# Three score products and the recurrence gates on 64 rows of the array instead of 128

## The chip, the cores and the metric

The program runs on one core of a Trainium2 chip. The metric is the device time of one execution in microseconds (us), as the median of three runs. Engines are named as in the profile: PE (TensorE, matmul), PEld (its weight loads), DVE (VectorE), ACT (ScalarE), POOL (GpSimd), SP (SyncE, which issues the weight DMAs).

## What is computed

A block of three layers over x of 256 positions by 1024 features, all in float32: a retention layer, a latent attention layer (16 heads) and a hybrid layer (a gated recurrence beside a sparse attention, then a feed-forward). Four products in it matter here; each sums over 64 features:

```python
# latent attention: 16 heads, 128 features of their own and 64 rotary ones, whose key is shared by all heads
sc = (jnp.einsum('bqhd,bkhd->bhqk', qn_i, k_nope)
      + jnp.einsum('bqhr,bkr->bhqk', qr_i, k_rope)).astype(jnp.float32) * scale
...
# recurrence gates: 16 blocks of 64 features, two matrices a block
xb = x.reshape(x.shape[:-1] + (RNN_BLOCKS, RNN_BLOCK_DIM))
y = jnp.einsum('btnd,nde->btne', xb, w)
...
# indexer: 8 heads of 64, one shared key
rel = jax.nn.relu(jnp.einsum('bqhd,bsd->bqhs', iqc, ik).astype(jnp.float32))
...
# sparse attention: 16 heads of 64, 4 key heads
s = jnp.einsum('bqgrd,bqkgd->bqgrk', qg, k_sel).astype(jnp.float32) * scale
```

## The kernel before

Each engine's program is written out by hand in its final order; engines meet through semaphores (`wait_ge`, `then_inc`). The large weights come as 148 units. For each unit SP loads `w_raw`, ACT copies it to `w_hi_ring` (`act_hi`, L932), DVE subtracts to get `w_lo_ring` (`dve_lo`, L1373), three units ahead of PE, and PE multiplies in three passes a tile (`mm3`, L337 to L339). Between the units PE does the small float32 products; PSUM has 8 banks of 512 columns.

Latent attention: 8 pairs of heads (`pe_pair`). While pair p is projected, pair p-1 is attended: the scores of head 0 into bank 5 after the gate unit, its transposes (`pe_turn_p`) into bank 6 two units later, then the scores of head 1 into bank 5. A head has four score matmuls (`pe_scores`, L612 and L613): 128 and 256 keys, each over the 128 own features and then over 128 rows of which 64 belong to the other head; `b_kr` holds the rotary key twice, with zeros in the other head's rows.

Hybrid layer, `pe_hybrid`: a loop of 16 units n=0 to 15, each 48 matmuls. Before units 0 and 1 stand four indexer heads each (L739, key padded with zeros in `c_ikz`), before units 2 and 3 four tiles of recurrence gates each (L746 and L747: one matmul per matrix, two 64-feature blocks on the diagonal of a 128x128 weight padded with zeros). After units 6, 8, 10 and 12 come the attention scores of key head g=0 to 3 (L759 and L761, keys padded in `c_kz`), after units 8, 10, 12, 14 the transposes of the exponentials of g=0 to 3 (L776), after the odd units 9 to 15 the values (L787). These transposes wait for `sc_exp`, the end of the exponentials on ACT (`act_attention_exps`, L1332), which wait for the maxima on DVE (`dve_attention_scores`, L1935 to L1944).

ACT's program in the same loop, for each n: the copy of unit n+3, then the indexer's relu (n<2), or the sigmoids of the gates (n=2, 3, L1315 and L1316, one activation of 128x256 each), or the recurrence's exp and tanh (n=4, L1246 and L1250) and sqrt (n=5), then what unit n itself left in its bank (gelu, L1263, for n<4; tanh, L1269, for n=4 to 11), then for n=6, 8, 10, 12 the exponentials. PE waits before unit n=2 to 5 for the gelu of unit n-2, before n=6 to 13 for the tanh of unit n-2. A change of function costs a table load.

Of the kernel before, what the change touches and what calls it, by code (L numbers as in the profile page):

```python
# [6 lines left out]
ACT = mybir.ActivationFunctionType  # L7
# [68 lines left out]
    "c_sq", "c_total", "c_h0", "c_h1", "c_drain_a", "c_drain_v", "c_kw_hi", "c_kw_lo", "c_sp_in", "c_sp_exp", "c_zeros",  # L76
# [110 lines left out]
def place_latent(k):  # L187
# [12 lines left out]
    k.b_kr = k.place("b_kr", [P, 2, S])  # L200
# [8 lines left out]
def place_hybrid(k):  # L209
# [6 lines left out]
    k.c_kz = k.place("c_kz", [P, HKV, S])  # L216
    k.c_iqT = k.place("c_iqT", [P, IH // 2, S])
    k.c_ikz = k.place("c_ikz", [P, 2, S])
# [6 lines left out]
    k.c_rgw = k.place("c_rgw", [P, 2, KD, P])  # L225
# [372 lines left out]
def pe_scores(k, pair, h):  # L598

    T, s, ps, par = k.T, k.s, k.ps, pair % 2  # L600
    i = 2 * pair + h
    if h == 0:
        T.wait_ge(s["b_qn"], pair + 1)
        T.wait_ge(s["b_kn"], pair + 1)
        T.wait_ge(s["b_qr"], pair + 1)
        T.wait_ge(s["b_v"], pair + 1)
        T.wait_ge(s["b_kr"], 1)
    if i:
        T.wait_ge(s["b_masked"], i)
# [28 lines left out]
def pe_pair(k, pair):  # L638
# [13 lines left out]
    else:  # L652
        pe_scores(k, pair - 1, 0)
# [36 lines left out]
def pe_attention_hooks(k):  # L690
# [13 lines left out]
    def last_split():  # L704
# [3 lines left out]
            1: [lambda: pe_scores(k, last, 0)],  # L708
            2: [lambda: pe_turn_p(k, last, 0), lambda: pe_scores(k, last, 1), outputs_split],
# [97 lines left out]
def pe_hybrid(k):  # L807
# [41 lines left out]
    for n in range(16):  # L849
# [7 lines left out]
        elif n in (2, 3):  # L857
# [3 lines left out]
            for c in range(4 * (n - 2), 4 * (n - 2) + 4):  # L861
                pe_recurrence_gates(k, 16 + c, c)
# [221 lines left out]
def act_pT(k, pair, h):  # L1084
# [4 lines left out]
    A.activation(k.b_pT[:, h, :], k.ps[:, 6, 0:3 * P], ACT.Copy).then_inc(s["b_pT"], 1)  # L1089
# [35 lines left out]
def act_attention_output(k):  # L1125
# [19 lines left out]
    act_dma(k, "rgw_in", k.c_rgw[:, :, :, :].rearrange("p a k n -> p (a k n)"), d["rg_w"])  # L1145
# [15 lines left out]
def act_hybrid(k):  # L1161
# [72 lines left out]
    for n in range(16):  # L1234
# [50 lines left out]
def act_to_features(k, i, name, t0):  # L1285
# [320 lines left out]
def dve_key_rotary(k):  # L1606
# [7 lines left out]
    for n in range(2):  # L1614
# [552 lines left out]
```

## Time and profile before

| | us |
|---|---|
| median of 3 runs | 912.55 (912.54 to 913.08) |
| profiled execution, device time | 912.84 |
| its span on the core | 911.5 |
| PE busy in the span | 903.1 (99%) |
| PEld, DVE, ACT, POOL busy | 812.8, 594.4, 494.7, 79.6 |
| granted TensorE clock, mean | 0.999 |

Outside the span lie 1.3 us (912.84 less 911.5). A row of the timeline gives the start of a group, its length, its engine, the line, the operation, output and inputs (moving operand first, then the weights), the array size, the moving shape, and in brackets the idle time before it. A float32 matmul stands as two records (x2), each with a weight load of its own. PE's records overlap: what counts is the distance from one start to the next.

### The profile page before, as it was taken

The page shows a single profiled execution, that of the slowest core. Times are in us where ns is not written, and L with a number is a line of the kernel's source. Part 1 is how long each engine was busy: PE and PEld are TensorE (multiplying, and loading weights), DVE is VectorE, ACT ScalarE, POOL GpSimd, SP SyncE. Part 2 cuts the span into 40 slices and gives each one's busy share as a digit, 9 for nine tenths or more (in the row PEclk, how much of TensorE's full clock was granted, in tenths as well). Part 3 has the DMA queues.
Part 4 walks back from the last instruction along what each step waited for, and adds up shares of the span by engine and source line. Part 5 has one row for each costly group of instructions (what it writes and reads, how often), then busy time and mean ns, then how long its engine had stood idle before and what let it go on. Part 6 is the DMA issues. An engine that isn't in the chain of part 4 may idle for free.

```text
span 911.5 us, 13482 instructions
## 1 busy us (share of the span) xinstructions
PE 903.1 (99%) x5671; PEld 812.8 (89%) x5671; DVE 594.4 (65%) x795; ACT 494.7 (54%) x624; POOL 79.6 (9%) x60
## 2 busy tenths in 40 slices
PE   9999999999999999999999999999999999999998
PEld 8798887888899999999877899999999888888887
DVE  5876656569866666666477788766657665566441
ACT  6444454436766666664437576877754355446330
POOL 0010110000001111111000000222200012211000
PEclk9999999999999999999999999999999999999999
DMA  9835464543544443354465444242244535445720
GB/s 351 324 124 177 182 228 155 194 150 122 185 185 145 145 145 145 145 186 185 160 236 198 171 146 178 93 140 93 97 181 164 206 139 185 164 161 212 253 110 24
DMA packets 24829, 154.65 MB, mean 170 GB/s; under 512 B 3136, under 2 KB 3520, under 8 KB 9024
## 3 DMA queue, kind: packets, MB, share of 16 engines
q1 hardware_dynamic: 22880, 148.97, 45.4%
q10 hardware_dynamic: 1728, 4.28, 1.5%
q8 instruction: 45, 0.74, 0.3%
q0 software_dynamic: 160, 0.52, 0.1%
q14 instruction: 16, 0.13, 0.0%
HBM read 152.72 MB, written 1.05 MB: 169 GB/s over the span
## 4 chain that ended last, share of the span: by engine, by line
PE 88%; ACT 5%; DVE 4%; issue 2%; DMA 1%; SPq 0%; ACTq 0%
PE ps L337 23%; PE ps L339 23%; PE ps L338 22%; PE ps L388 7%; PE ps L391 3%; ACT w_hi_ring L932 1%; ACT c_p L1332 1%; PE ps L612 1%; PE ps L613 1%; PE ps L633 1%; DMA w_raw<-in_a_w_in 1%; PE ps L410 1%; PE ps L517 1%; PE ps L623 1%; PE ps L787 1%
## 5 line engine op out<-in xcount | busy, mean ns | idle before, releaser
L1373 DVE TENSOR_TENSOR w_lo_ring<-w_raw,w_hi_ring 128x2048 fp32r<-128x2048 f32 x146 | 341.8, 2353 | 201.3 <-ACT w_hi_ring L932 201.1
L932 ACT ACTIVATE w_hi_ring<-w_raw 128x2048 fp32r<-128x2048 f32 x146 | 277.4, 1909 | 109.8 <-PE ps L339 104.3
L337 PE MATMUL ps<-xT_hi,w_hi_ring 128*128 128x256 f32 x520 | 149.8, 288 | 0.6 <-DVE w_lo_ring L1379 0.5
L339 PE MATMUL ps<-xT_hi,w_lo_ring 128*128 128x256 f32 x520 | 147.0, 283 | 0.0
L338 PE MATMUL ps<-xT_lo,w_hi_ring 128*128 128x256 f32 x520 | 147.0, 283 | 0.0
L337 PE MATMUL ps<-w_hi_ring,xT_hi 128*128 128x512 f32 (+1 forms) x272 | 107.5, 395 | 1.4 <-DVE xT_lo L1550 0.6
L339 PE MATMUL ps<-w_hi_ring,xT_lo 128*128 128x512 f32 (+1 forms) x272 | 104.5, 384 | 0.0
L338 PE MATMUL ps<-w_lo_ring,xT_hi 128*128 128x512 f32 (+1 forms) x272 | 104.2, 383 | 0.0
L337 PEld LDWEIGHTS ps<-xT_hi,w_hi_ring 128*128 128x128 f32 x520 | 99.6, 192 | 2.2 <-issue 1.5
L338 PEld LDWEIGHTS ps<-xT_lo,w_hi_ring 128*128 128x128 f32 x520 | 99.6, 192 | 0.7
L339 PEld LDWEIGHTS ps<-xT_hi,w_lo_ring 128*128 128x128 f32 x520 | 99.6, 192 | 0.0
L388 PE MATMUL ps<-xw,w_hi_ring 128*128 128x512 f32 x256 | 80.5, 396 | 0.0
L337 PEld LDWEIGHTS ps<-w_hi_ring,xT_hi 128*128 128x128 f32 x272 | 51.1, 188 | 12.6 <-issue 2.3
L339 PEld LDWEIGHTS ps<-w_hi_ring,xT_lo 128*128 128x128 f32 x272 | 51.0, 188 | 9.8
L338 PEld LDWEIGHTS ps<-w_lo_ring,xT_hi 128*128 128x128 f32 x272 | 51.1, 188 | 9.5 <-issue 1.0
L391 PEld LDWEIGHTS ps<-xw,w_lo_ring 128*128 128x128 f32 x256 | 48.1, 188 | 11.4
L391 PE MATMUL ps<-xw,w_lo_ring 128*128 128x256 f32 x256 | 50.3, 278 | 0.0
L337 PE MATMUL ps<-w_hi_ring,c_fT_hi 128*128 128x512 f32 x128 | 49.9, 390 | 0.0
L339 PE MATMUL ps<-w_hi_ring,c_fT_lo 128*128 128x512 f32 x128 | 49.8, 389 | 0.0
L338 PE MATMUL ps<-w_lo_ring,c_fT_hi 128*128 128x512 f32 x128 | 49.8, 389 | 0.0
L337 PE MATMUL ps<-b_qlatT_hi,w_hi_ring 128*128 128x256 f32 x144 | 41.9, 291 | 0.0
L339 PE MATMUL ps<-b_qlatT_hi,w_lo_ring 128*128 128x256 f32 x144 | 40.4, 281 | 0.0
(327 smaller groups left out, 1704.9 us busy)
## 6 DMA issues: line engine op xcount, KB each, us to landing
w_raw<-in_a_w_in SPq DMA_DIRECT2D x22, 1024.0 KB, 5.0
w_raw<-in_w_ff_in SPq DMA_DIRECT2D x16, 1024.0 KB, 4.8
w_raw<-in_w_ff_out SPq DMA_DIRECT2D x16, 1024.0 KB, 4.8
w_raw<-in_b_w_uq SPq DMA_DIRECT2D x16, 576.0 KB, 4.5
w_raw<-in_a_w_out SPq DMA_DIRECT2D x8, 1024.0 KB, 4.9
w_raw<-in_b_w_gate SPq DMA_DIRECT2D x8, 1024.0 KB, 4.8
w_raw<-in_kv_w_up SPq DMA_DIRECT2D x8, 1024.0 KB, 4.8
w_raw<-in_b_w_out SPq DMA_DIRECT2D x8, 1024.0 KB, 4.8
```

The lines of the kernel that those rows point to most:

```text
L337: k.T.matmul(out, lh, rh, start=start, stop=False, skip_group_check=True)
L338: k.T.matmul(out, lh, rl, start=False, stop=False, skip_group_check=True)
L339: return k.T.matmul(out, ll, rh, start=False, stop=stop, skip_group_check=True)
L388: k.T.matmul(out, wh[:, n, c * P:(c + 1) * P], xw[:, n, :, :].rearrange("p a s -> p (a s)"), start=n == 0, stop=False, skip_group_check=True)
L391: m = k.T.matmul(out[:, 0:S], wl[:, n, c * P:(c + 1) * P], xw[:, n, 0, :], start=False, stop=n == KD - 1, skip_group_check=True)
L410: m = k.T.transpose(bank[:, (2 * n + t) * P:(2 * n + t + 1) * P], src(t, 2 * pair + n), k.ident[:, :])
L517: m = T.matmul(k.ps[:, 0, cols], k.a_qk[:, 2 + n, e * P:(e + 1) * P], k.a_qk[:, n, e * P:2 * P], start=e == 0 and n == 0, stop=n == 1, ski ...
L612: T.matmul(out, k.b_qn[:, par, h, qs], k.b_kn[:, par, h, keys], start=q == 0, stop=False, skip_group_check=True)
L613: m = T.matmul(out, k.b_qr[:, par, qs], k.b_kr[:, h, keys], start=False, stop=True, skip_group_check=True)
L623: m = T.transpose(k.ps[:, 6, n * P:(n + 1) * P], k.b_p[:, h, n * P:(n + 1) * P], k.ident[:, :])
L932: k.A.activation(k.hi[:, u % RING, :], k.raw[u % RING][:, :], ACT.Copy).then_inc(k.s["w_hi"], 1)
L1373: k.V.tensor_tensor(k.lo[:, u % RING, :], k.raw[u % RING][:, :], k.hi[:, u % RING, :].bitcast(F32), ALU.subtract).then_inc(k.s["w_lo"], 1)
```

## The change

The products over 64 features address only 64 of the 128 rows: rows 0 to 63 or 64 to 127, where the operands lie. No zeros are stored, and the memsets of `b_kr`, `c_kz` and `c_ikz` go. Matmuls on opposite halves are issued in turn, with outputs in different banks.

- Latent attention: the scores of both heads are issued together, before the first q unit, into banks 5 and 6; first the four matmuls over 128 rows, then four over 64. The transposes go back into the same head's bank.
- Indexer: a head uses the half its features lie in.
- Gates: a 64-feature block has both matrices side by side, 64 columns each, as one 64-row by 128-column weight. Two banks serve two tiles (`pair`); the two halves of a tile come out in different banks, so the sigmoids work on 64 partitions each, twice as many of them.
- Sparse attention: heads keep their order; `c_kT` holds each key head in both halves, eight copies of 64x256 instead of four. Eight matmuls alternate between the halves, and before (r, q) = (1, 0) PE waits for its own (2, 0) (`sc_even`), since both write bank 4.

```diff
-    k.b_kr = k.place("b_kr", [P, 2, S])
+    k.b_kr = k.place("b_kr", [P, 2, S])[:, 0, :]
...
-    k.c_kz = k.place("c_kz", [P, HKV, S])
+    k.c_kT = k.place("c_kT", [P, HKV, S])
     k.c_iqT = k.place("c_iqT", [P, IH // 2, S])
-    k.c_ikz = k.place("c_ikz", [P, 2, S])
+    k.c_ikT = k.place("c_ikT", [P, 2, S])[:, 0, :]
...
-    k.c_rgw = k.place("c_rgw", [P, 2, KD, P])
+    k.c_rgw = k.place("c_rgw", [P, 2, KD, P])[:, 0, :, :]
...
-def pe_scores(k, pair, h):
+def pe_scores(k, pair):
 
     T, s, ps, par = k.T, k.s, k.ps, pair % 2
-    i = 2 * pair + h
-    if h == 0:
-        T.wait_ge(s["b_qn"], pair + 1)
-        T.wait_ge(s["b_kn"], pair + 1)
-        T.wait_ge(s["b_qr"], pair + 1)
-        T.wait_ge(s["b_v"], pair + 1)
-        T.wait_ge(s["b_kr"], 1)
-    if i:
-        T.wait_ge(s["b_masked"], i)
-    for q, cols in enumerate((slice(0, P), slice(P, 3 * P))):
-        out, qs, keys = ps[:, 5, cols], slice(q * P, (q + 1) * P), slice(0, (q + 1) * P)
-        T.matmul(out, k.b_qn[:, par, h, qs], k.b_kn[:, par, h, keys], start=q == 0, stop=False, skip_group_check=True)
-        m = T.matmul(out, k.b_qr[:, par, qs], k.b_kr[:, h, keys], start=False, stop=True, skip_group_check=True)
-    m.then_inc(s["b_scored"], 1)
+    T.wait_ge(s["b_qn"], pair + 1)
+    T.wait_ge(s["b_kn"], pair + 1)
+    T.wait_ge(s["b_qr"], pair + 1)
+    T.wait_ge(s["b_v"], pair + 1)
+    T.wait_ge(s["b_kr"], 1)
+    if pair:
+        T.wait_ge(s["b_pT"], 2 * pair)
+    spans = [(slice(q * P, (q + 1) * P), slice(0, (q + 1) * P), cols) for q, cols in enumerate((slice(0, P), slice(P, 3 * P)))]
+    for h in range(2):
+        for qs, keys, cols in spans:
+            T.matmul(ps[:, 5 + h, cols], k.b_qn[:, par, h, qs], k.b_kn[:, par, h, keys], start=qs.start == 0, stop=False,
+                     skip_group_check=True)
+    for qs, keys, cols in spans:
+        for h in range(2):
+            rows = slice(h * ROPE, (h + 1) * ROPE)
+            m = T.matmul(ps[:, 5 + h, cols], k.b_qr[rows, par, qs], k.b_kr[rows, keys], start=False, stop=True,
+                         skip_group_check=True)
+            if qs.start:
+                m.then_inc(s["b_scored"], 1)
 
 
 def pe_turn_p(k, pair, h):
     T, s, i = k.T, k.s, 2 * pair + h
     T.wait_ge(s["b_p"], i + 1)
-    if i:
-        T.wait_ge(s["b_pT"], i)
     for n in range(3):
-        m = T.transpose(k.ps[:, 6, n * P:(n + 1) * P], k.b_p[:, h, n * P:(n + 1) * P], k.ident[:, :])
+        m = T.transpose(k.ps[:, 5 + h, n * P:(n + 1) * P], k.b_p[:, h, n * P:(n + 1) * P], k.ident[:, :])
     m.then_inc(s["b_pturned"], 1)
...
     else:
-        pe_scores(k, pair - 1, 0)
+        pe_scores(k, pair - 1)
...
         pe_turn_p(k, pair - 1, 0)
-        pe_scores(k, pair - 1, 1)
...
-            1: [lambda: pe_scores(k, last, 0)],
-            2: [lambda: pe_turn_p(k, last, 0), lambda: pe_scores(k, last, 1), outputs_split],
+            1: [lambda: pe_scores(k, last)],
+            2: [lambda: pe_turn_p(k, last, 0), outputs_split],
...
+def half_rows(n):
+    return slice(64 * (n % 2), 64 * (n % 2) + 64)
 def pe_index_scores(k, i, hd):
-    bank = pe_small_bank(k, i)
+    bank, rows = pe_small_bank(k, i), half_rows(hd)
     for q, cols in enumerate(QCOLS):
-        m = k.T.matmul(bank[:, cols], k.c_iqT[:, hd // 2, q * P:(q + 1) * P], k.c_ikz[:, hd % 2, 0:(q + 1) * P],
+        m = k.T.matmul(bank[:, cols], k.c_iqT[rows, hd // 2, q * P:(q + 1) * P], k.c_ikT[rows, 0:(q + 1) * P],
                        start=q == 0, stop=True, skip_group_check=True)
     m.then_inc(k.s["small_mm"], 1)
 
 
-def pe_recurrence_gates(k, i, n):
-    bank = pe_small_bank(k, i)
-    k.T.matmul(bank[:, 0:S], k.c_rgw[:, 0, n, :], k.c_xc[:, n, :], start=True, stop=True, skip_group_check=True)
-    k.T.matmul(bank[:, S:2 * S], k.c_rgw[:, 1, n, :], k.c_xc[:, n, :], start=False, stop=True,
-               skip_group_check=True).then_inc(k.s["small_mm"], 1)
+def pe_recurrence_gates(k, i, pair):
+    banks = [pe_small_bank(k, i + n) for n in range(2)]
+    for c in range(2):
+        for n in range(2):
+            rows, tile = half_rows(n), 2 * pair + c
+            m = k.T.matmul(banks[n][:, c * S:(c + 1) * S], k.c_rgw[rows, tile, :], k.c_xc[rows, tile, :], start=c == 0, stop=True,
+                           skip_group_check=True)
+            if c == 1:
+                m.then_inc(k.s["small_mm"], 1)
 
 
 def pe_attention_scores(k, g):
...
         T.wait_ge(s["sc_in"], g)
     else:
         T.wait_ge(s["small_read"], 24)
-    for r in range(4):
-        tile = 4 * (g // 2) + r
-        T.matmul(ps[:, 4, r * P:(r + 1) * P], k.c_qT[:, tile, 0:P], k.c_kz[:, g, 0:P], start=r == 0, stop=True,
-                 skip_group_check=True)
-        m = T.matmul(ps[:, 5 + r // 2, (r % 2) * S:(r % 2 + 1) * S], k.c_qT[:, tile, P:2 * P], k.c_kz[:, g, :],
-                     start=r % 2 == 0, stop=True, skip_group_check=True)
+    for r, q in ((0, 0), (1, 1), (2, 0), (3, 1), (0, 1), (1, 0), (2, 1), (3, 0)):
+        if (r, q) == (1, 0):
+            T.wait_ge(s["sc_even"], g + 1)
+        rows, tile = half_rows(r), 2 * g + r // 2
+        out = ps[:, 5 + r % 2, (r // 2) * S:(r // 2 + 1) * S] if q else ps[:, 4, r * P:(r + 1) * P]
+        m = T.matmul(out, k.c_qT[rows, tile, q * P:(q + 1) * P], k.c_kT[rows, g, 0:(q + 1) * P],
+                     start=r < 2 if q else r == 0, stop=True, skip_group_check=True)
+        if (r, q) == (2, 0):
+            m.then_inc(s["sc_even"], 1)
     m.then_inc(s["sc_mm"], 1)
...
-            for c in range(4 * (n - 2), 4 * (n - 2) + 4):
-                pe_recurrence_gates(k, 16 + c, c)
+            for pair in range(2 * (n - 2), 2 * (n - 2) + 2):
+                pe_recurrence_gates(k, 16 + 2 * pair, pair)
...
-    A.activation(k.b_pT[:, h, :], k.ps[:, 6, 0:3 * P], ACT.Copy).then_inc(s["b_pT"], 1)
+    A.activation(k.b_pT[:, h, :], k.ps[:, 5 + h, 0:3 * P], ACT.Copy).then_inc(s["b_pT"], 1)
...
         for g in range(HKV):
-            rows = slice(64 * (g % 2), 64 * (g % 2) + 64)
-            m = A.activation(k.c_kz[rows, g, :], bank[rows, (g // 2) * S:(g // 2 + 1) * S], ACT.Copy, scale=hn[rows, 1:2])
+            src = half_rows(g)
+            for n in range(2):
+                m = A.activation(k.c_kT[half_rows(n), g, :], bank[src, (g // 2) * S:(g // 2 + 1) * S], ACT.Copy, scale=hn[src, 1:2])
     else:
-        A.wait_ge(s["c_zeros"], 1)
-        for g in range(2):
-            rows = slice(64 * g, 64 * g + 64)
-            m = A.activation(k.c_ikz[rows, g, :], bank[rows, 0:S], ACT.Copy, scale=hn[rows, 2:3])
+        m = A.activation(k.c_ikT, bank[:, 0:S], ACT.Copy, scale=hn[:, 2:3])
     m.then_inc(s["small_read"], 1)
...
-def act_recurrence_gates(k, i, n):
-    A, s, bank = k.A, k.s, k.ps[:, 4 + i % 4, :]
-    A.wait_ge(s["small_mm"], i + 1)
-    A.activation(k.c_rr[:, n, :], bank[:, 0:S], ACT.Sigmoid, bias=k.vec["rg_ba_2"][:, n:n + 1])
-    A.activation(k.c_ig[:, n, :], bank[:, S:2 * S], ACT.Sigmoid, bias=k.vec["rg_bx_2"][:, n:n + 1]).then_inc(s["small_read"], 1)
+def act_recurrence_gates(k, i, pair):
+    A, s, vec = k.A, k.s, k.vec
+    for n in range(2):
+        A.wait_ge(s["small_mm"], i + n + 1)
+        bank, own, other = k.ps[:, 4 + (i + n) % 4, :], half_rows(n), half_rows(n + 1)
+        for c in range(2):
+            tile, cols = 2 * pair + c, slice(c * S, (c + 1) * S)
+            A.activation(k.c_rr[own, tile, :], bank[own, cols], ACT.Sigmoid, bias=vec["rg_ba_2"][own, tile:tile + 1])
+            m = A.activation(k.c_ig[own, tile, :], bank[other, cols], ACT.Sigmoid, bias=vec["rg_bx_2"][other, tile:tile + 1])
+        m.then_inc(s["small_read"], 1)
 
 
 def head_scale(k, g):
 
-    first = 8 * (g // 2) + g % 2
-    return k.c_qs[:, :, first:first + 7:2]
+    return k.c_qs[:, :, 4 * g:4 * g + 4]
...
-    own.mark(V.memset(k.b_kr[:, :, :], 0.0))
...
-    for n in range(2):
-        rows = slice(n * ROPE, (n + 1) * ROPE)
-        m = V.tensor_tensor(k.b_kr[rows, n, :], k.b_xc[rows, :], k.b_xs[rows, :], ALU.add)
-    m.then_inc(s["b_kr"], 1)
+    V.tensor_tensor(k.b_kr, k.b_xc[:, :], k.b_xs[:, :], ALU.add).then_inc(s["b_kr"], 1)
...
-        m = V.tensor_tensor(q1[:, 2 * half:2 * half + 2, :], ps[:, 5 + half, :].rearrange("p (k s) -> p k s", k=2),
+        m = V.tensor_tensor(q1[:, half:half + 3:2, :], ps[:, 5 + half, :].rearrange("p (k s) -> p k s", k=2),
...
-    G.wait_ge(s["c_kw_lo"], 1)
-    G.memset(k.c_kz[:, :, :], 0.0)
-    G.memset(k.c_ikz[:, :, :], 0.0).then_inc(s["c_zeros"], 1)
...
-    rg = np.zeros((P, 2, KD, P), wa.dtype)
-    for n, w in enumerate((wa, wx)):
-        for half in range(2):
-            rows = slice(64 * half, 64 * half + 64)
-            rg[rows, n, :, rows] = w[half::2].transpose(1, 0, 2)
+    rg = np.empty((P, KD, P), wa.dtype)
+    for half in range(2):
+        rows, other = slice(64 * half, 64 * half + 64), slice(64 * (1 - half), 64 * (1 - half) + 64)
+        rg[rows, :, rows] = wa[half::2].transpose(1, 0, 2)
+        rg[rows, :, other] = wx[half::2].transpose(1, 0, 2)
     out["rg_w"] = rg.reshape(P, -1)
```

PE in the latent attention, pair p-1's scores between the gate unit and the end of the two q units of pair p. `b_kn`, `b_qn` are the own features, `b_kr`, `b_qr` the rotary ones, `b_p` the softmax of a head. Before, with the 54 matmuls of the q units left out:

```order
L612 MATMUL ps<-b_kn,b_qn 128x128 [waits b_v,b_qr,b_kr,b_kn,b_qn]
L613 MATMUL ps<-b_kr,b_qr 128x128
L612 MATMUL ps<-b_kn,b_qn 128x256
L613 MATMUL ps<-b_kr,b_qr 128x256
...
L623 MATMUL ps<-ident,b_p 128x128 [waits b_p]
L623 MATMUL ps<-ident,b_p 128x128 x2
L612 MATMUL ps<-b_kn,b_qn 128x128 [waits b_masked]
L613 MATMUL ps<-b_kr,b_qr 128x128
L612 MATMUL ps<-b_kn,b_qn 128x256
L613 MATMUL ps<-b_kr,b_qr 128x256
```

After, the same stretch:

```order
L611 MATMUL ps<-b_kn,b_qn 128x128 [waits b_v,b_qr,b_kr,b_kn,b_qn]
L611 MATMUL ps<-b_kn,b_qn 128x256
L611 MATMUL ps<-b_kn,b_qn 128x128
L611 MATMUL ps<-b_kn,b_qn 128x256
L616 MATMUL ps<-b_kr,b_qr 128x128 x2
L616 MATMUL ps<-b_kr,b_qr 128x256 x2
...
L626 MATMUL ps<-ident,b_p 128x128 [waits b_p]
L626 MATMUL ps<-ident,b_p 128x128 x2
```

Head 1's scores moved ahead of the q units, and the rotary matmuls of both heads stand in a row of four; the number of matmuls is the same.

ACT in the hybrid loop, n=2: the sigmoids before the gelu of unit 2. `c_rr` and `c_ig` are the two gates. Before:

```order
L1315 ACTIVATE c_rr<-ps,c_columns 128x256 [waits small_mm]
L1316 ACTIVATE c_ig<-ps,c_columns 128x256
L1315 ACTIVATE c_rr<-ps,c_columns 128x256 [waits small_mm]
L1316 ACTIVATE c_ig<-ps,c_columns 128x256
...
L1263 ACTIVATE c_gel<-ps 128x512 [waits w_used]
```

After:

```order
L1337 ACTIVATE c_rr<-ps,c_columns 64x256 [waits small_mm]
L1339 ACTIVATE c_ig<-ps,c_columns 64x256
L1337 ACTIVATE c_rr<-ps,c_columns 64x256
L1339 ACTIVATE c_ig<-ps,c_columns 64x256
L1337 ACTIVATE c_rr<-ps,c_columns 64x256 [waits small_mm]
L1339 ACTIVATE c_ig<-ps,c_columns 64x256
L1337 ACTIVATE c_rr<-ps,c_columns 64x256
L1339 ACTIVATE c_ig<-ps,c_columns 64x256
...
L1282 ACTIVATE c_gel<-ps 128x512 [waits w_used]
```

Eight activations of 128 partitions ahead of the gelu became sixteen of 64, in units 2 and 3 alike.

## Rows read from the trace of the kernel before

**Rows 1.** The page, busy time of each engine.

```profile
PE 903.1 (99%) x5671; PEld 812.8 (89%) x5671; DVE 594.4 (65%) x795; ACT 494.7 (54%) x624; POOL 79.6 (9%) x60
```

**Rows 2.** The page, chain that ended last, by engine.

```profile
PE 88%; ACT 5%; DVE 4%; issue 2%; DMA 1%; SPq 0%; ACTq 0%
```

**Rows 3.** The same chain in order of time, 560 to 690 us: start, length, what.

```profile
560.71 2.62 PE ps L739 x16
...
569.08 0.43 PE ps L746 x2
...
588.01 1.91 ACT w_hi_ring L932
...
591.23 3.32 ACT c_aa L1246 x8
...
605.79 1.81 ACT w_hi_ring L932
...
665.21 2.62 PE ps L787 x24
```

**Rows 4.** Timeline of PE, 286 to 300 us: latent attention, one head's scores.

```profile
289.53 0.38 PE L612 MATMUL ps<-b_kn,b_qn 128*128 128x128 f32 x2
289.75 0.39 PE L613 MATMUL ps<-b_kr,b_qr 128*128 128x128 f32 x2
289.98 0.60 PE L612 MATMUL ps<-b_kn,b_qn 128*128 128x256 f32 x2
290.41 0.59 PE L613 MATMUL ps<-b_kr,b_qr 128*128 128x256 f32 x2
...
290.96 0.28 PE L338 MATMUL ps<-b_qlatT_lo,w_hi_ring 128*128 128x256 f32 x1
```

**Rows 5.** Timeline of PE, 598 to 690 us: the four transposes of exponentials.

```profile
618.74 1.53 PE L776 MATMUL ps<-ident,c_p 128*128 128x128 f32 x12
...
636.90 1.47 PE L776 MATMUL ps<-ident,c_p 128*128 128x128 f32 x12
...
655.39 1.53 PE L776 MATMUL ps<-ident,c_p 128*128 128x128 f32 x12 [0.37 <-ACT c_p L1332]
...
673.33 1.47 PE L776 MATMUL ps<-ident,c_p 128*128 128x128 f32 x12
```

**Rows 6.** Timeline of ACT, 530 to 690 us: last record of each key head's exponentials.

```profile
618.50 0.19 ACT L1332 ACTIVATION_READ_ACCUMULATOR c_p<-c_p,c_few,c_qs 128x1 f32 x1
...
636.08 0.19 ACT L1332 ACTIVATION_READ_ACCUMULATOR c_p<-c_p,c_few,c_qs 128x1 f32 x1
...
655.15 0.19 ACT L1332 ACTIVATION_READ_ACCUMULATOR c_p<-c_p,c_few,c_qs 128x1 f32 x1
...
670.39 0.19 ACT L1332 ACTIVATION_READ_ACCUMULATOR c_p<-c_p,c_few,c_qs 128x1 f32 x1
```

**Rows 7.** The same timeline of ACT: units 1 to 3 of the hybrid loop.

```profile
569.11 0.60 ACT L1263 ACTIVATE c_gel<-ps 128x512 f32<-128x512 f32 x1 [4.45 <-PE ps L339]
...
572.82 0.48 ACT L1315 ACTIVATE c_rr<-ps,c_columns 128x256 f32<-128x256 f32 x1
...
575.87 1.28 ACT L1263 ACT_TABLE_LOAD   x1
578.31 0.60 ACT L1263 ACTIVATE c_gel<-ps 128x512 f32<-128x512 f32 x1 [1.16 <-PE ps L339]
...
587.51 0.60 ACT L1263 ACTIVATE c_gel<-ps 128x512 f32<-128x512 f32 x1 [1.16 <-PE ps L339]
```

**Rows 8.** ACT's half-row activations, instructions of line 1295, then the timeline.

```profile
L1295 ACT ACTIVATE c_kz<-ps,c_columns x4: 470/470/472, 549.7 to 551.1; 64x256 f32<-64x256 f32 x4
...
549.66 1.92 ACT L1295 ACTIVATE c_kz<-ps,c_columns 64x256 f32<-64x256 f32 x4
552.38 1.02 ACT L1231 ACTIVATE c_xc<-ps,c_columns 128x256 f32<-128x256 f32 x2 [0.80 <-PE ps L339]
```

More of the change, by code:

```diff
@@ L74 @@
     "b_pturned", "b_pT", "b_valued", "b_og", "b_oT_hi", "b_oT_lo", "b_qn", "b_cos", "b_sin", "b_qr", "b_kn", "b_v",
-    "c_sq", "c_total", "c_h0", "c_h1", "c_drain_a", "c_drain_v", "c_kw_hi", "c_kw_lo", "c_sp_in", "c_sp_exp", "c_zeros",
+    "c_sq", "c_total", "c_h0", "c_h1", "c_drain_a", "c_drain_v", "c_kw_hi", "c_kw_lo", "c_sp_in", "c_sp_exp", "sc_even",
     "c_ikw_mm", "c_ikw", "c_heads", "c_conv0", "c_conv", "small_mm", "small_read", "ix_acc", "selected",
@@ L1144, in act_attention_output @@
     act_dma(k, "kw_in", k.c_kw_raw[:, :, :].rearrange("p k n -> p (k n)"), d["w_ikw"])
-    act_dma(k, "rgw_in", k.c_rgw[:, :, :, :].rearrange("p a k n -> p (a k n)"), d["rg_w"])
+    act_dma(k, "rgw_in", k.c_rgw.rearrange("p k n -> p (k n)"), d["rg_w"])
     act_hi(k, U_BOUT + 6 + AHEAD)
@@ L1239, in act_hybrid @@
         elif n < 4:
-            for c in range(4 * (n - 2), 4 * (n - 2) + 4):
-                act_recurrence_gates(k, 16 + c, c)
+            for pair in range(2 * (n - 2), 2 * (n - 2) + 2):
+                act_recurrence_gates(k, 16 + 2 * pair, pair)
         elif n == 4:
@@ L1627, in dve_softmax @@
     for q, cols in enumerate(qcols):
-        m = V.tensor_tensor_reduce(out=k.b_p[:, h, cols], in0=ps[:, 5, cols], in1=k.b_mask[:, cols], scale=SCALE_B, scalar=-3.0e38,
+        m = V.tensor_tensor_reduce(out=k.b_p[:, h, cols], in0=ps[:, 5 + h, cols], in1=k.b_mask[:, cols], scale=SCALE_B, scalar=-3.0e38,
                                    op0=ALU.add, op1=ALU.max, accum_out=k.b_sums[:, h, q:q + 1])
@@ L2095, in layout @@
     rnn_x, rnn_g, q, k, v, iq, ik, iw, gates = np.split(w, np.cumsum([DR, DR, D, 256, 256, IH * ID, ID, IH]), 1)
-    group = HC // HKV
-    order = [(t // group * 2 + half) * group + t % group for t in range(HC // 2) for half in range(2)]
-    q = q.reshape(D, HC, DC)[:, order].reshape(D, D)
     out["w_qkvi"] = units(np.concatenate([q, k, v, iq], 1), 4, 512)
@@ L2111, in layout @@
     out["head_norms"] = np.ascontiguousarray(np.stack(norms, 1))
+    out["rg_bx_2"] = np.roll(out["rg_bx_2"], 64, 0)
     out["columns"] = np.ascontiguousarray(np.concatenate([out.pop(name) for name, _ in COLUMNS_C], 1))
     wa, wx = out.pop("rg_wa_2")[0], out.pop("rg_wx_2")[0]
-    rg = np.zeros((P, 2, KD, P), wa.dtype)
-    for n, w in enumerate((wa, wx)):
-        for half in range(2):
-            rows = slice(64 * half, 64 * half + 64)
-            rg[rows, n, :, rows] = w[half::2].transpose(1, 0, 2)
+    rg = np.empty((P, KD, P), wa.dtype)
[3 more added lines that the diff above has]
+        rg[rows, :, other] = wx[half::2].transpose(1, 0, 2)
     out["rg_w"] = rg.reshape(P, -1)
```

## The prediction

> **What bounds the kernel now.** I read the page first: PE is busy 903.1 of 911.5 us, no other engine over 65% [rows 1], and the chain that ended last is 88% PE [rows 2]. So a microsecond taken from PE is worth one, unless another engine stands right behind it. The chain in order of time says where one does: from 588.01 us it leaves PE for ACT and DVE (first the copy of a weight unit, then the recurrence's exp, a later copy) and comes back to PE only at the transposes at 655.39 [rows 3, 5]. PE itself shows 0.37 us of idle time there [rows 5], which hides how close the race is. To measure it I set the end of each key head's exponentials beside the start of PE's transposes of them [rows 5, 6]: for g=0 the last record ends at 618.50 + 0.19 = 618.69 and PE starts at 618.74, slack none; for g=1 636.27 against 636.90, slack 0.6; for g=2 655.34 against 655.39, and PE had waited; for g=3 670.58 against 673.33, slack 2.7. So between unit 3 of the hybrid loop and the third transposes, ACT and DVE set the pace as much as PE does. Before that PE leads: ACT's gelus wait for PE 4.45 us in unit 1 and 1.16 us each in units 2 and 3 [rows 7].
>
> **What 64 rows can save on PE.** A float32 matmul is two records. From start to start a matmul of 128 moving columns takes 0.22 us and one of 256 takes 0.43 [rows 4], so 0.11 and 0.215 a record. The trace of before has no matmul on part of the rows, so what two halves do together has to be bounded. No overlap: nothing is saved. Full overlap of opposite halves: half. I take the middle: records start in order, and the second record of one matmul runs beside the first of the next one on the other half, while the two records of one matmul, on one half, follow each other. I also let no two records start closer than 0.11 us, since the 24 records of values, with only 64 moving columns each, still take 2.62 us, 0.109 each [rows 3], which I read as the time of a weight load.
> - Rotary scores of a pair: before 2 x (0.22 + 0.43) = 1.30 us. After, eight records: 8 x 0.11 = 0.88. Saved 0.42.
> - Indexer, four heads: before 2.62 [rows 3]. Each head ends in a record of 0.215 that the next head's two short ones run beside: 2.62 - 3 x 0.215 = 1.98. Saved 0.64, twice.
> - Gates of a unit: before 8 x 0.43 = 3.44 [rows 3]; after 9 x 0.215 = 1.94. Saved 1.5, twice.
> - Attention scores of a key head: before 4 x (0.22 + 0.43) = 2.6; after, by the weight loads, 16 x 0.11 = 1.76. Saved 0.86, four times.
>
> **Switches.** Going from 128 to 64 rows and back may cost something each time; no row shows it. Below: nothing. Above: what a matmul still takes after the next could start, 0.28 - 0.12 or 0.38 - 0.22 = 0.16 us [rows 4] (the 0.12 is three passes of a unit in 0.36, a 48-matmul unit thus 5.75), plus one uncovered weight load of 0.11, so 0.27. I take 0.11, the load alone, the nearest thing with a row. Two switches go with each group. The Trainium skill ("TensorEngine Tiling (Array Packing)", Key Properties) says that changing the tiling mode drains the engine; no run here shows it. By it alone the switch would be 0.16 and my sum 1.2 us higher.
>
> **Latent attention.** Eight pairs, (0.42 - 0.22) each: -1.6 us. It lies on PE's path: the scores' inputs come from the pair before, through engines that start from PE's own end of the values, so nothing new is waited for. The wait for `b_masked` goes, the new one for `b_pT` is for a copy that PE's values of the pair before already waited for. The softmax of head 0 still has the two q units (54 x 0.12 = 6.5 us) before its transposes; head 1's is early. The DVE memset and the split add are off the path: nothing.
>
> **Hybrid, up to unit 1.** Indexer: 2 x (0.64 - 0.22) = -0.84 us. ACT has eight key copies in place of four and one indexer copy in place of two: five times 0.48 less two, +1.4 us, in front of a convolution drain that ACT was 0.8 us early for [rows 8]; the next gelu had still more room. Nothing on the path. The POOL memsets were long done.
>
> **Hybrid, units 2 and 3: the gates move the bound to ACT.** Before, eight sigmoids lie between 572.82 and the table load at 575.87, 3.05 us [rows 7], some 0.36 apart. After there are sixteen, on 64 partitions. The nearest rows are the four copies of 64x256: 470 ns each, the four in 1.92, so 0.48 apart, with no overlap between them [rows 8]. Sixteen at 0.48 are 7.7 us, 4.65 more in each of the two units. ACT's idle time in them, 1.16 each [rows 7], is used up first: 2 x 4.65 - 2.3 = +7.0 us at the gelu of unit 3. PE arrives 3 us early there and gets nothing for it. From that gelu ACT runs without a gap through the copy at 588.01, the exp at 591.23, tanh, sqrt and their table loads to the copy at 605.79 [rows 3], DVE takes over, and the exponentials of g=0 end at 618.69. All of it starts from the gelu and moves by 7.0. PE waits before units 5 and 6 (gelu of unit 3, tanh of unit 4) and again at the transposes. Lower bound for an activation: 0.36 as for the full-row sigmoids, 16 x 0.36 = 5.8, and ACT is +3.4 late instead of +7.0.
> The Trainium skill ("ScalarE: Activation LUTs", What ACT_TABLE_LOAD costs) has back-to-back activations overlap by about 93 ns; the full-row sigmoids do so, the half-row copies of rows 8 don't. With it the late start would be the smaller one, rival 1 below.
>
> **Hybrid, from there.** The exponentials of g=1 and g=2 follow those of g=0 by 17.6 and 19.1 us [rows 6] on ACT and DVE alone. The scores' saving, 0.86 - 0.22 = 0.64 each, is lost where PE waits: after g=2 PE still stands at +7.0. Between the third and the fourth transposes PE leads again (slack 2.7), and one saving counts: +7.0 - 0.64 = +6.4. The rest of the kernel moves as a whole.
>
> **Sum.** -1.6 - 0.84 + 6.4 = +3.9 us (rounded). The profiled execution took 912.84 and the median is 912.55, 0.3 lower; with the change 912.84 + 3.9 = 916.7, on the median's scale **916.5 us**. With free switches: +7.0 - 0.86 - 1.28 - 3.36 = +1.5, 914.0. With 0.27 a switch: 7.0 - 0.3 - 0.2 + 1.0 = +7.5, 920.1.
>
> **The rivals.**
> 1. *Half-row sigmoids overlap as full-row ones do* (0.36 us). ACT is +3.4 late. With my switch: 3.4 - 0.64 - 0.84 - 1.6 = +0.3, 912.9. With free switches: 3.4 - 5.5 = -2.1, **910.4, faster**. This is the case on the other side: it needs both, sigmoids under about 0.37 us apart and switches near zero. For it: the sigmoids of before. Against: the only half-row rows there are.
> 2. *No overlap of the halves in float32.* PE saves nothing and pays the switches: 7.0 + 0.2 + 0.4 + 1.8 = +9.4, 922.0; with free switches 919.5. For it: two records and two weight loads a matmul, each load 0.11. Against: records and loads already overlap on the full array.
> 3. *Full overlap.* A group takes half: 1.3, 2.6 and 5.2 us (one score group, both indexer groups, eight pairs). With my switch 7.0 - 1.1 - 2.2 - 3.4 = +0.3, 912.8; free, 7.0 - 9.2 = -2.2, 910.4; with sigmoids at 0.36 as well 906.8 to 909.3. It needs a matmul to start beside the whole of the one before; the order of two records each speaks against that. The Trainium skill ("TensorE: Matmul & The Clock Gate", Part 3) gives such starts some 4 ns apart on separate row groups; no run here shows that.
>
> **How the numbers follow.** My forecast, with any switch cost, 0.47; rival 1 0.22; rival 2 0.13; rival 3 0.18. A measurement of this kernel can tell about 0.2%, 1.8 us, from no change. Faster: rival 1 with free switches 0.07, rival 3 in part 0.10, together 0.17. Within 0.2% (910.7 to 914.4): my case with free switches 0.12, rival 1 0.12, rival 3 0.08, together 0.32. Slower: 0.51. The range from 910.5 to 920.6 leaves out most of rival 2 and the best of rival 3, 0.2 in all.
>
> **What would show it.** Half-row sigmoids 0.48 or 0.36 apart in the timeline of ACT; no idle time on ACT ahead of the gelus of units 2 and 3; the gelu of unit 3 later behind that of unit 1 than 18.4 us before, by 7.0. PE idle ahead of units 5 and 6, several us in all, released by ACT. Eight rotary records in 0.9 us and the gap behind them; 1.8 us from the first to the last attention score. Slack between exponentials and transposes near zero for g=0 and g=2. The forecast is wrong if PE shows no idle time ahead of unit 6, or if records on opposite halves don't start beside each other.

## The result and the profile after

The change makes the kernel slower: 915.24 us (median of nine runs, 914.75 to 915.59) against 912.54 (nine runs, 912.24 to 913.30). The ratio is 1.0028, 95% interval 1.0019 to 1.0037. The profiled execution took 915.06 us with a span of 913.7.

The page of the changed kernel, busy times and chain, against [rows 1, 2]:

```profile
PE 897.3 (98%) x5671; PEld 800.8 (88%) x5671; DVE 593.3 (65%) x793; ACT 504.8 (55%) x643; POOL 78.1 (9%) x58
...
PE 85%; ACT 7%; DVE 4%; issue 2%; DMA 1%; SPq 0%; ACTq 0%
```

PE has 5.8 us less to do in a span 2.2 us longer; ACT has 10.1 us more, and its share of the chain went from 5 to 7%. Who waited for whom, PE's waits (total, times, longest), shows two that were not there before:

```profile
PE ps L337 <- ACT c_g L1288: 4.8, 2, 4.5
PE ps L759 <- ACT c_ig L1339: 2.7, 1, 2.7
```

Of the first, 4.5 us stand ahead of unit 6 of the hybrid loop, for the tanh of unit 4. The second is inside the gates of unit 3, whose last tiles need banks that the sigmoids haven't read yet.

**Where ACT's time goes.** The timeline of ACT, units 1 to 3, against [rows 7]:

```profile
565.12 0.60 ACT L1282 ACTIVATE c_gel<-ps 128x512 f32<-128x512 f32 x1 [3.63 <-PE ps L339]
...
568.83 0.47 ACT L1337 ACTIVATE c_rr<-ps,c_columns 64x256 f32<-64x256 f32 x1
569.31 0.47 ACT L1339 ACTIVATE c_ig<-ps,c_columns 64x256 f32<-64x256 f32 x1
569.79 0.47 ACT L1337 ACTIVATE c_rr<-ps,c_columns 64x256 f32<-64x256 f32 x1
...
576.58 1.28 ACT L1282 ACT_TABLE_LOAD   x1
577.87 0.60 ACT L1282 ACTIVATE c_gel<-ps 128x512 f32<-128x512 f32 x1
...
590.62 0.60 ACT L1282 ACTIVATE c_gel<-ps 128x512 f32<-128x512 f32 x1
```

The sixteen sigmoids stand 0.48 us apart and take 7.75 us to the table load (568.83 to 576.58), where eight took 3.05. The gelus of units 2 and 3 no longer wait for PE. The gelu of unit 3 follows that of unit 1 by 25.50 us; before, by 18.40. That is +7.1.

**What the halves do on PE.** Timeline of PE, latent attention. The first two rows show the whole groups, 128 rows and then 64; the next two show the first two records of 128 columns and the last two of 256 inside the second group; then comes the step back to 128 rows:

```profile
289.01 1.47 PE L611 MATMUL ps<-b_kn,b_qn 128*128 128x128 f32 x8
290.42 0.93 PE L616 MATMUL ps<-b_kr,b_qr 64*128 64x128 f32 x8
...
290.42 0.38 PE L616 MATMUL ps<-b_kr,b_qr 64*128 64x128 f32 x2
...
290.96 0.38 PE L616 MATMUL ps<-b_kr,b_qr 64*128 64x256 f32 x2
291.27 0.39 PE L337 MATMUL ps<-b_qlatT_hi,w_hi_ring 128*128 128x256 f32 x1
291.50 0.28 PE L338 MATMUL ps<-b_qlatT_lo,w_hi_ring 128*128 128x256 f32 x1
```

In each of the x2 rows of L616 two records together take the 0.38 us of one: those of opposite halves start 6 to 7 ns apart by the trace's time stamps. So the halves overlap completely. Changing to 64 rows and back costs on both sides: the last record on 128 rows starts at 290.11 and is due 0.215 later, and the rotary ones begin at 290.42, 0.10 late; at the other end 290.96 + 0.215 gives 291.18, and the unit begins at 291.27. Behind each change the first record is also 0.11 longer than usual: 291.27 to 291.50 is 0.23 in place of 0.12. That makes 0.21 a change.

**Where PE and ACT meet.** The timeline of ACT has the last record of the exponentials of g=0, against [rows 6]:

```profile
621.59 0.19 ACT L1355 ACTIVATION_READ_ACCUMULATOR c_p<-c_p,c_few,c_qs 128x1 f32 x1
```

The timeline of PE has the four transposes, against [rows 5]:

```profile
623.26 1.47 PE L795 MATMUL ps<-ident,c_p 128*128 128x128 f32 x12
...
640.46 1.47 PE L795 MATMUL ps<-ident,c_p 128*128 128x128 f32 x12
...
658.51 1.53 PE L795 MATMUL ps<-ident,c_p 128*128 128x128 f32 x12 [0.46 <-ACT c_p L1355]
...
675.53 1.47 PE L795 MATMUL ps<-ident,c_p 128*128 128x128 f32 x12
```

The account by stations, in us after the change less before: gelu of unit 1 -4.0 (565.12 against 569.11: latent attention and indexer), gelu of unit 3 +3.1 (that is -4.0 + 7.1), end of the exponentials of g=0 +3.1, third transposes +3.1, fourth +2.2, span +2.2. At g=0 PE comes 1.5 us after the exponentials, which I had not forecast. The reason is in this view, the granted clock in three stretches of 4 us (after the length: busy time of PE, PE's weight loads, DVE, ACT and POOL, each with its count; then the granted clock, where 1.00 is 2.4 GHz and 0.50 is 1.2, the DMA share and GB/s):

```profile
598.00:602.00 4.00, 0.26 (x1) 0.26 (x2) 3.90 (x8) 4.00 (x11) 0.00 (x0) 0.82 0.53 223
602.00:606.00 4.00, 4.00 (x20) 4.00 (x21) 2.79 (x2) 3.97 (x3) 0.00 (x0) 0.50 0.00 0
606.00:610.00 4.00, 4.00 (x30) 4.00 (x29) 0.00 (x0) 3.97 (x5) 3.21 (x1) 0.83 0.76 262
```

PE had been idle 4.46 us before 601.74, as its timeline has it; after that the clock stood at its lower level and unit 6 took 8.4 us (601.74 to 610.15), not 5.8.

```profile
601.74 0.58 PE L337 MATMUL ps<-xT_hi,w_hi_ring 128*128 128x256 f32 x1 [4.46 <-ACT c_g L1288]
```

There is a second such stretch, behind the wait inside the gates of unit 3; the timeline of PE has

```profile
576.70 1.23 PE L759 MATMUL ps<-c_xc,c_rgw 64*128 64x256 f32 x4 [2.69 <-ACT c_ig L1339]
```

and the view of the granted clock

```profile
576.00:580.00 4.00, 3.30 (x14) 2.57 (x15) 0.00 (x0) 3.96 (x5) 0.00 (x0) 0.58 0.02 4
```

What PE loses there is taken up by its idle time ahead of unit 6.

### The profile page after: what moved, and what is told of

It is laid out like the page before. It is cut to its first block, busy times and chain, and to the rows that moved or that the text cites. A ratio compares the mean times of both kernels' runs of the same rounds, so it can differ in the third digit from the quotient of the medians.

```text
span 913.7 us, 13486 instructions
## 1 busy us (share of the span) xinstructions
PE 897.3 (98%) x5671; PEld 800.8 (88%) x5671; DVE 593.3 (65%) x793; ACT 504.8 (55%) x643; POOL 78.1 (9%) x58
## 4 chain that ended last, share of the span: by engine, by line
PE 85%; ACT 7%; DVE 4%; issue 2%; DMA 1%; SPq 0%; ACTq 0%
PE ps L337 22%; PE ps L339 22%; PE ps L338 22%; PE ps L388 7%; PE ps L391 3%; ACT w_hi_ring L951 2%; ACT c_p L1355 1%; PE ps L611 1%; PE ps L636 1%; DMA w_raw<-in_a_w_in 1%; ACT c_rr L1337 1%; PE ps L616 1%; ACT c_ig L1339 1%; PE ps L410 1%; PE ps L517 1%
```

## The experiments

The theory: PE gains everywhere, and the sixteen half-row sigmoids take it back through ACT's chain, more than once over. Its rivals: the loss lies in the changes between 128 and 64 rows, in the eight key copies, or in the clock. Each time below stands beside runs of the kernel before on the same chip (912.79, 913.1, 912.75 us in the three sets).

**The gates put back.**

```diff
-    for pair in range(2 * (n - 2), 2 * (n - 2) + 2):
-        act_recurrence_gates(k, 16 + 2 * pair, pair)
+    for c in range(4 * (n - 2), 4 * (n - 2) + 4):
+        act_recurrence_gates(k, 16 + c, c)
...
-    k.c_rgw = k.place("c_rgw", [P, 2, KD, P])[:, 0, :, :]
+    k.c_rgw = k.place("c_rgw", [P, 2, KD, P])
```

> The changed kernel with the gates alone put back (full-row matmuls over the padded weight, eight sigmoids of 128x256 a unit); both score changes and the latent attention stay. If the sixteen half-row sigmoids are the loss, the gelu of unit 3 comes 18.4 us after that of unit 1 again, not 25.5, everything behind moves 7.1 us earlier up to the third transposes, and the kernel gains what the rest is worth: 912.5 - 2.3 (latent attention) - 1.7 (indexer) - 0.9 (last score group) = 907.6 us. If the loss comes from something else (the switches of the scores, the eight key copies), the time stays at 915 or goes up by the 3 to 4 us that PE now spends on the gates.

Measured 908.70 us, ratio 0.9957 (0.9944 to 0.9969): faster than both kernels. The gelu of unit 3 follows that of unit 1 by 18.40 us again:

```profile
565.69 0.60 ACT L1276 ACTIVATE c_gel<-ps 128x512 f32<-128x512 f32 x1 [3.63 <-PE ps L339]
574.89 0.60 ACT L1276 ACTIVATE c_gel<-ps 128x512 f32<-128x512 f32 x1 [1.16 <-PE ps L339]
584.09 0.60 ACT L1276 ACTIVATE c_gel<-ps 128x512 f32<-128x512 f32 x1 [1.16 <-PE ps L339]
```

So the gates cost 6.8 us of the changed kernel (+2.7 against -4.1, each beside its own runs of the kernel before), though PE spends more on them in this version: from the first gate matmul to the second matmul of the unit behind it 3.57 us, in the changed kernel's unit 2 it is 2.15. That is some 2.8 us in two units, not the 3 to 4 of the forecast. Of the 1.1 us by which the time misses the forecast, about half is the latent attention, next but one, and 0.3 that the kernel before is itself slower beside these runs (912.79).

**The gates alone.**

```diff
-def act_recurrence_gates(k, i, n):
+def act_recurrence_gates(k, i, pair):
...
+            A.activation(k.c_rr[own, tile, :], bank[own, cols], ACT.Sigmoid, bias=vec["rg_ba_2"][own, tile:tile + 1])
```

> The kernel before with the gates alone changed. If the sigmoids are the loss: +7.1 us at the gelu of unit 3 and 919.7 us in all. PE then idles over 4 us ahead of unit 6 and, as in the changed kernel, may run unit 6 at the lower clock level, 2.4 us longer; with the scores at their old length there is less slack to take that up, and then it reaches the transposes: 921.6 us. If the shorter PE work counted, it would be 912.5 - 4 = 908.5 us.

Measured 921.19 us, ratio 1.0089 (1.0074 to 1.0104): 8.4 slower than before, not 7.1. The exponentials of g=2 end 7.1 us later after the gelu of unit 1 than before, but PE starts the third transposes 1.9 us behind them (663.94 against 662.04). That fits the second forecast, in which the slow unit 6 shows; whether it is the clock is asked further down.

**The latent attention alone.**

```diff
+            m = T.matmul(ps[:, 5 + h, cols], k.b_qr[rows, par, qs], k.b_kr[rows, keys], start=False, stop=True,
```

> The kernel before with the latent attention alone changed. The start-to-start time of a pair falls from 23.06 us by 0.31, as the two traces show, and nothing stands behind PE there: 912.5 - 2.4 = 910.1 us. If a wait in the attention or the hybrid part gives it back, 912.5 us.

Measured 910.95 us, ratio 0.998 (0.9971 to 0.9989): -1.8. From pair to pair PE now takes 22.84 us, before 23.06, so 0.22 less; in the profile of the changed kernel it was 22.75, with the same instructions. I had read 0.31 from that one execution, and it was 0.1 too much, eight times.

**Indexer and attention scores alone.**

```diff
+        m = k.T.matmul(bank[:, cols], k.c_iqT[rows, hd // 2, q * P:(q + 1) * P], k.c_ikT[rows, 0:(q + 1) * P],
...
+        m = T.matmul(out, k.c_qT[rows, tile, q * P:(q + 1) * P], k.c_kT[rows, g, 0:(q + 1) * P],
```

> The kernel before with the indexer and the attention scores alone changed. Indexer: 2 x (1.31 - 0.42) = 1.8 us ahead of the gelus, kept. Scores: 0.9 us each in four groups, of which only the last counts if ACT and DVE set the pace up to the third transposes: 912.5 - 1.8 - 0.9 = 909.8 us. If all four count: 907.2 us. Together with the latent attention alone it should add up to the kernel with the old gates.

Measured 910.32 us, ratio 0.9972 (0.9962 to 0.9983): -2.5, close to the -2.7 in which three of the four score groups bring nothing, and far from -5.3. With the latent attention the parts make -4.3; both together, the first experiment, -4.1. The parts add up. The key copies are in this kernel and cost nothing.

PE's waits in it say where the other three savings went, 2.8 us in all; the 1.3 stand ahead of unit 11:

```profile
PE ps L787 <- ACT c_p L1341: 1.5, 3, 0.8
...
PE ps L337 <- ACT c_g L1280: 1.3, 1, 1.3
```

**The sigmoids in another order.** Both of one half of a bank, then both of the other.

```diff
+        for c in range(2):
+            tile, cols = 2 * pair + c, slice(c * S, (c + 1) * S)
+            A.activation(k.c_rr[own, tile, :], bank[own, cols], ACT.Sigmoid, bias=vec["rg_ba_2"][own, tile:tile + 1])
         for c in range(2):
             tile, cols = 2 * pair + c, slice(c * S, (c + 1) * S)
-            A.activation(k.c_rr[own, tile, :], bank[own, cols], ACT.Sigmoid, bias=vec["rg_ba_2"][own, tile:tile + 1])
             m = A.activation(k.c_ig[own, tile, :], bank[other, cols], ACT.Sigmoid, bias=vec["rg_bx_2"][other, tile:tile + 1])
```

> The changed kernel with each bank's four sigmoids in another order: the two of one gate (same half of the bank), then the two of the other. If an activation on 64 partitions never overlaps the one before, all stay 0.48 us apart and the time is 915.2. If it is the change of the half from one to the next that costs, the second of each two comes 0.36 us behind the first: 8 x 0.12 = 1.0 us less a unit, 913.3.

Measured 914.19 us, ratio 1.0011 (1.0002 to 1.0021), so 1.6 us less loss than the whole change against the runs beside it. PE's program is the same as in the changed kernel, so this part of the loss is ACT's alone: the gelu of unit 3 follows that of unit 1 by 23.56 us, not 25.50. Timeline of ACT:

```profile
569.04 0.83 ACT L1337 ACTIVATE c_rr<-ps,c_columns 64x256 f32<-64x256 f32 x2
569.88 0.83 ACT L1340 ACTIVATE c_ig<-ps,c_columns 64x256 f32<-64x256 f32 x2
570.74 0.83 ACT L1337 ACTIVATE c_rr<-ps,c_columns 64x256 f32<-64x256 f32 x2
```

Two of 0.47 in 0.83 us: the second starts 0.36 behind the first, as full-row sigmoids do. From group to group it is 0.84 to 0.86, so 0.48 to 0.50 from the second to the next. It is not the 64 partitions that keep activations from overlapping; it is the change of the half, on the input side (569.04 group to 569.88) as well as on the output side (569.88 to 570.74). Rows 8 had copies that changed the half each time.

**PE kept busy ahead of unit 6.** The extra products are read by nobody.

```diff
+            if n == 6:
+                T.wait_ge(s["small_read"], 24)
+                wait_lo(k, T, U_MAIN + n)
+                for _ in range(20):
+                    T.matmul(ps[:, 7, :], k.hi[:, (U_MAIN + n) % RING, 0:P], k.hi[:, (U_MAIN + n) % RING, 0:512], start=True, stop=True,
```

> The changed kernel with 20 extra matmuls of 512 columns, read by nobody, on PE in the 4.5 us in which it waits ahead of unit 6. The granted clock should stay at the upper level through units 6 and 7, unit 6 take 5.8 us in place of 8.2, and PE reach the first transposes some 1 us before the exponentials of g=0 end instead of 1.4 us behind them. If the slow unit 6 is hidden by the slack ahead of the second and third transposes, the time stays at 915.2. If it is part of the loss, 912.8.

Measured 916.09 us, ratio 1.0031 (1.002 to 1.0042): no gain over 1.0028. The clock did stay up in unit 6, here from 602 to 608 us (the stretch behind the gates of unit 3 stays slow, 0.72 from 576 to 582):

```profile
602.00:608.00 6.00, 6.00 (x50) 5.81 (x48) 3.20 (x2) 5.95 (x5) 0.77 (x1) 1.00 0.11 18
```

And PE's waits hold this one for the exponentials:

```profile
PE ps L795 <- ACT c_p L1361: 1.6, 3, 0.9
```

PE then arrives early at all of the first three transposes and waits 1.6 us for the exponentials. From the gelu of unit 1 to the third transposes it is 93.4 us with the extra matmuls and 93.4 without. In the changed kernel the slow unit 6 costs nothing.

**The same with the gates alone.** The same lines, added to the second experiment's kernel.

```diff
+            if n == 6:
...
+                for _ in range(20):
+                    T.matmul(ps[:, 7, :], k.hi[:, (U_MAIN + n) % RING, 0:P], k.hi[:, (U_MAIN + n) % RING, 0:512], start=True, stop=True,
```

> The kernel before with the gates alone changed (921.2 us), and the 20 extra matmuls ahead of unit 6. There the first transposes start 2.5 us behind the exponentials of g=0 and the third 1.9 us behind theirs, so the slow unit 6 is not hidden. If the clock is what costs there, the third transposes follow the exponentials at once and the time falls by 1.9 us, to 919.3. If it is not, it stays at 921.2.

Measured 920.22 us, ratio 1.0083 (1.0066 to 1.01), 1.0 lower than without the extra matmuls; the intervals overlap, so by the times alone it is open. The traces are clearer: the third transposes now wait for the exponentials,

```profile
662.02 1.53 PE L787 MATMUL ps<-ident,c_p 128*128 128x128 f32 x12 [0.39 <-ACT c_p L1355]
```

where they started at 663.94 without a wait; both kernels have their gelu of unit 1 at 568.6 to 568.7, and the spans are 919.9 and 918.4. The profiled execution of this kernel is the fastest of its four, so 1.5 us is at the upper end. The lower clock of unit 6 costs 1.0 (medians) to 1.5 us (traces) where the scores keep their old length, and nothing where they are short.

**Eight changes of rows a pair in place of two.**

```diff
-    for h in range(2):
-        for qs, keys, cols in spans:
-            T.matmul(ps[:, 5 + h, cols], k.b_qn[:, par, h, qs], k.b_kn[:, par, h, keys], start=qs.start == 0, stop=False,
-                     skip_group_check=True)
     for qs, keys, cols in spans:
         for h in range(2):
             rows = slice(h * ROPE, (h + 1) * ROPE)
+            T.matmul(ps[:, 5 + h, cols], k.b_qn[:, par, h, qs], k.b_kn[:, par, h, keys], start=qs.start == 0, stop=False,
+                     skip_group_check=True)
             m = T.matmul(ps[:, 5 + h, cols], k.b_qr[rows, par, qs], k.b_kr[rows, keys], start=False, stop=True,
```

> The changed kernel with the latent scores in the order own, rotary, own, rotary: eight changes between 128 and 64 rows a pair in place of two, and no two matmuls on opposite halves in a row. If a change costs the 0.21 us that the trace shows (0.10 of gap, 0.11 of a weight load that nothing covers), a pair's scores take 2.62 + 8 x 0.21 = 4.3 us in place of 2.37, 8 x 1.9 = 15 us in all: 930.6. If only the gap is paid, 922 to 924. If changes cost nothing, 915.2 + 8 x 0.65 = 917.5 at most, less what they cost now.

Measured 930.63 us, ratio 1.0189 (1.0172 to 1.0206), the time that 0.21 us a change gives; to the tenth it is luck, since beside its own runs of the kernel before (913.1) it lies 14.8 us above the changed kernel and not 15.4. From pair to pair PE takes 24.66 us, and 23.06 in the kernel before: 1.60 us for eight changes, 0.20 each. The timeline of PE has a head's own and rotary matmuls of 128 keys 0.31 and 0.41 us apart, where both took 0.22 before [rows 4]:

```profile
291.55 0.38 PE L612 MATMUL ps<-b_kn,b_qn 128*128 128x128 f32 x2
291.86 0.48 PE L614 MATMUL ps<-b_kr,b_qr 64*128 64x128 f32 x2
292.27 0.49 PE L612 MATMUL ps<-b_kn,b_qn 128*128 128x128 f32 x2
292.69 0.48 PE L614 MATMUL ps<-b_kr,b_qr 64*128 64x128 f32 x2
```

The Trainium skill ("TensorEngine Tiling (Array Packing)", Key Properties) says that a change of mode drains the engine. The trace agrees that there is a gap, 0.10 us; with the uncovered weight load the price is twice that.

**A version that beats both.** The first experiment still had PE waiting 1.4 us at the transposes and 1.3 for a tanh. The forecast below puts the 1.3 ahead of unit 6, and that is misread. PE has no idle time there; the wait stands ahead of unit 11, for the tanh of unit 9, which ACT does after the exponentials of g=1:

```profile
637.24 0.38 PE L337 MATMUL ps<-xT_hi,w_hi_ring 128*128 128x256 f32 x1 [1.28 <-ACT c_g L1282]
```

Two steps moved:

```diff
             m.then_inc(s["rec_exp"], 1)
+            act_gate_tanh(k, n)
             A.wait_ge(s["rec_exp"], 1)
...
-        if n < 15:
+        late = n in (6, 8, 10, 12)
+        if n < 15 and not late:
             dve_lo(k, U_MAIN + n + AHEAD)
...
             dve_attention_scores(k, (n - 6) // 2)
+            dve_lo(k, U_MAIN + n + AHEAD)
```

> The changed kernel with the old gates, as in the first of these experiments, and two steps moved: ACT does the tanh of unit 4 between the recurrence's exp and tanh, not behind both, and DVE takes in the attention scores of a key head before its copy of the weight unit of the same n, not after. There PE idles 1.3 us ahead of unit 6 and 1.4 us ahead of the transposes, both behind ACT and DVE. If that is all that keeps PE back, 908.7 - 2.7 = 906.0 us. If the weight units that now come later hold PE up in their turn, 908.7 us or more.

Measured 905.39 us, ratio 0.9918 (0.9904 to 0.9933). The timeline of ACT, last record of the exponentials of g=0:

```profile
611.01 0.19 ACT L1352 ACTIVATION_READ_ACCUMULATOR c_p<-c_p,c_few,c_qs 128x1 f32 x1
```

The timeline of PE, the transposes of g=0 and of g=2:

```profile
614.34 1.47 PE L789 MATMUL ps<-ident,c_p 128*128 128x128 f32 x12
...
648.59 1.47 PE L789 MATMUL ps<-ident,c_p 128*128 128x128 f32 x12
```

PE no longer waits there; the slack at g=0 is 3.1 us (611.20 to 614.34). From 560 to 676 us its timeline has no idle time of PE, so the later weight units don't hold it up. All four score groups now count: from the gelu of unit 1 to the third transposes it is 82.9 us (565.65 to 648.59), 3.3 less than before (86.3), about three groups of 0.9 and the 0.37 that PE waited there. The gain over the first experiment is 3.3 us, 0.6 more than I forecast. The exponentials of g=0 end 4.1 us earlier than there (611.20 against 615.26). Since PE did not wait ahead of unit 6, the DVE step is the likelier cause; the two were not run apart, nor was either in the kernel before.

## Why the prediction was right, point by point

- *What bounds the kernel.* Right. The race of ACT and DVE with PE up to the third transposes is what decided the sign: a PE 5.8 us less busy in a slower kernel.
- *Gates move the bound to ACT, +7.0.* Right, by the row I took: 0.48 us apart, +7.1 from the gelu of unit 1 to that of unit 3. Putting the gates back removes it. The lower bound of 0.36 (rival 1) did not occur, though the order of the sigmoids brings half of them there.
- *What 64 rows save.* Here the step failed that let a matmul start beside only the second record of the one before. Full overlap, rival 3, is what happened: eight rotary records in 0.65 us of streaming, not 0.88. The floor of 0.11 us between starts doesn't hold across halves either. The Trainium skill ("TensorE: Matmul & The Clock Gate", Part 3) has starts about 4 ns apart on separate row groups, and the trace agrees but for the size, 6 to 7 ns in the latent attention and 13 in the indexer.
- *Switches.* Mis-sized, 0.20 to 0.21 us and not 0.11. Gap and load add; I took one of them. The two errors nearly cancel in the latent attention (-1.8 measured, -1.6 forecast), and that is luck: what happened is rival 3 with a switch twice as dear. In the indexer they don't cancel. With both heads fully beside each other it would be 2 x (1.31 - 0.42) = -1.8; the kernel with the indexer and scores alone has the gelu of unit 1 1.65 us earlier (567.46 against 569.11), against the -0.84 of the forecast. The last score group brings 0.9 against 0.64.
- *Sum.* +7.1 - 1.8 - 1.65 - 0.9 = +2.75, measured +2.7; the forecast of +3.9 is 1.2 too high, most of it the indexer.
- *From there on.* The exponentials of g=1 and g=2 followed by 17.6 and 19.1 us again, and only the last score group counted, as said. What I had missed is the clock: I forecast several us of idle time ahead of unit 6 but not that unit 6 would then run at the lower level. It had no price because the shorter scores left room; with the gates alone it had one.
- *A wait I didn't price:* 2.7 us inside the gates of unit 3, for banks the slower sigmoids hold. It and the lower clock behind it lie beside ACT's own delay; PE is idle again for 4.5 us ahead of unit 6, so neither shows in the time. Ahead of unit 5, where I forecast idle time too, there are only 0.2 us.

## What to carry to other kernels

Before halving an operation on the bound engine, ask how its output is laid out for the engine that drains it: two halves in different banks mean twice as many activations, each paying its fixed time. Group products on half of the rows so that a group has one change in and one out, some 0.4 us together, and don't use it for less than about 0.9 us of full-row work (an estimate: full overlap saves half of the work, two changes cost 0.42). Where a chain of other engines runs level with the bound engine, savings inside that stretch are lost until the chain itself is shortened; moving two steps brought 3.3 us here, and the array work without the gates 4.1 ahead of it.

## What the hardware showed unexpectedly

- In these traces the two halves of the array behave as two queues. In the indexer's program a head's two matmuls (128 and 256 columns, four records, all on one half) come before the next head's. In the trace four records of 128 columns come first and then four of 256, and the first two start 13 ns apart:

```profile
549.91 0.39 PE L747 MATMUL ps<-c_ikT,c_iqT 64*128 64x128 f32 x2
```

  So taking turns in the program isn't needed for two matmuls in a row on a half.
- Activations of 64x256 overlap by about 0.11 us with the one before as long as both work on the same half of the partitions, at input and output; where the half changes, they don't (0.36 and 0.48 us apart).
- After 4.46 us of idle time PE's clock was at its lower level (0.50 granted from 602 to 606 us) for most of the next unit, 2.6 us lost; 20 matmuls that nobody reads kept it up. After 2.69 us of idle time in the gates of unit 3 it was there too (0.58 from 576 to 580). With the old gates, where the longest wait in the loop is 1.28 us, the mean granted clock is 1.0.
